# Two padding tiles: the raw weights and their low halves start 32 bytes later in SBUF, everything behind them 128 bytes later

## The reference

```
h = x
proj = rms_norm(h) @ w_in            # 1024 x 2048, 1024 x 4096, 1024 x 7584
... branches ...
h = h + y @ w_out                    # 1024 x 1024
f = rms_norm(h) @ [w_gate, w_up]     # 1024 x 2816 each
h = h + (silu(gate) * up) @ w_down   # 2816 x 1024
```

## The kernel before

| tile | start before | mod 64 | mod 256 |
|---|---|---|---|
| `weights_raw`, `weights_lo`, `weights_near` | 16576 | 0 | 192 |
| `weights_hi` | 41152 | 0 | 192 |
| `act_F_hi`, `act_F_lo` | 104064, 112256 | 0 | 128 |
| `ffn_F_hi`, `ffn_F_lo` | 120448, 142976 | 0 | 128 |
| `conv_F_hi`, `conv_F_lo` | 193152, 197248 | 0 | 128 |
| `mla_F_hi`, `mla_F_lo` | 122624, 126720 | 0 | 0 |
| `weights_hi_more`, `weights_raw_more` and `weights_lo_more` | 208576, 216768 | 0 | 192 |
| `z_T` | 128640 | 0 | 128 |
| `a_probs_T`, `v_T` (plain float32) | 171648, 136832 | 0 | 128 |
| `r_qk_F` (plain float32) | 193056 | 32 | 32 |
| `conv_acc_F` | 139488 | 32 | 224 |

## Time and profile before

### The profile page before, as it was taken

One profiled execution on the slowest core, in us unless ns is written; L12 is line 12 of the kernel. 1 busy time (PEld: TensorE's weight loads), 2 busy tenths in 40 slices (PEclk: granted clock), 3 DMA queues, 4 the chain that ended last, 5 costly groups with the idle time before them and its releaser, 6 DMA issues.

```text
span 1235.8 us, 19035 instructions
## 1 busy us (share of the span) xinstructions
PE 1205.2 (98%) x7597; PEld 1013.5 (82%) x7597; DVE 901.5 (73%) x1463; ACT 639.1 (52%) x1034; POOL 100.4 (8%) x163
## 2 busy tenths in 40 slices
PE   7999999999999999999999999999999999999998
PEld 3566778888988788787999987988788787999986
DVE  7998877757589998687666655589997687665553
ACT  4334565665556665545444544556575545444441
POOL 6300011101000200201000001000200201000000
PEclk9999999999999999999999999999999999999999
DMA  7635666434565555354766664565445355565552
GB/s 251 221 94 173 205 208 191 156 119 146 163 205 168 155 157 187 133 169 164 216 201 188 193 195 154 174 211 169 158 153 188 132 170 170 190 197 193 191 194 75
DMA packets 71958, 215.68 MB, mean 175 GB/s; under 512 B 16256, under 2 KB 19744, under 8 KB 71744
## 3 DMA queue, kind: packets, MB, share of 16 engines
q1 hardware_dynamic: 65008, 206.37, 52.0%
q0 software_dynamic: 2112, 6.97, 1.8%
q10 hardware_dynamic: 4752, 1.14, 0.4%
HBM read 208.95 MB, written 3.15 MB: 172 GB/s over the span
## 4 chain that ended last, share of the span: by engine, by line
PE 86%; DVE 8%; ACT 3%; issue 2%; POOL 1%; DMA 0%; DVEq 0%; POOLq 0%; ACTq 0%
PE acc L700 17%; PE acc L702 17%; PE acc L701 17%; PE acc L678 7%; PE acc L680 7%; PE acc L679 7%; PE acc L639 3%; PE mixed L1015 1%; DVE weights_lo L1776 1%; PE mixed L1112 1%; ACT junk L1279 1%; PE turned L755 1%; DVE h_T L1806 1%; PE mixed L999 1%; PE mixed L1008 1%
## 5 line engine op out<-in xcount | busy, mean ns | idle before, releaser
L1776 DVE TENSOR_TENSOR weights_lo<-weights_raw,weights_hi 128x1024 fp32r<-128x1024 f32 (+1 forms) x304 | 355.7, 1204 | 71.6 <-ACT weights_hi L1244 71.0
L1244 ACT ACTIVATE weights_hi<-weights_raw 128x1024 fp32r<-128x1024 f32 (+1 forms) x304 | 305.8, 1043 | 80.8 <-DMA weights_raw<-stream_dram 80.6
L700 PE MATMUL acc<-weights_hi,act_F_hi 128*128 128x512 f32 (+1 forms) x680 | 275.7, 406 | 5.6 <-DVE act_F_lo L1806 3.4
L702 PE MATMUL acc<-weights_hi,act_F_lo 128*128 128x512 f32 (+1 forms) x680 | 267.2, 393 | 0.0
L701 PE MATMUL acc<-weights_lo,act_F_hi 128*128 128x512 f32 (+1 forms) x680 | 265.4, 390 | 0.0
L678 PE MATMUL acc<-act_F_hi,weights_hi 128*128 128x256 f32 x624 | 173.6, 278 | 0.0
L679 PE MATMUL acc<-act_F_hi,weights_lo 128*128 128x256 f32 x624 | 172.5, 276 | 0.0
L680 PE MATMUL acc<-act_F_lo,weights_hi 128*128 128x256 f32 x624 | 172.4, 276 | 0.0
L700 PEld LDWEIGHTS acc<-weights_hi,act_F_hi 128*128 128x128 f32 x680 | 128.7, 189 | 34.2 <-DVE act_F_lo L1806 4.3
L702 PEld LDWEIGHTS acc<-weights_hi,act_F_lo 128*128 128x128 f32 x680 | 128.4, 189 | 28.4
L701 PEld LDWEIGHTS acc<-weights_lo,act_F_hi 128*128 128x128 f32 x680 | 128.7, 189 | 25.6
(11 more groups left out here) (339 smaller groups left out, 1923.6 us busy)
## 6 DMA issues: line engine op xcount, KB each, us to landing
weights_raw<-stream_dram SPq DMA_DIRECT2D x306, 512.0 KB, 3.7
weights_raw_more<-stream_dram SPq DMA_DIRECT2D x58, 512.0 KB, 4.3
gains<-rows_dram POOLq DMA_DIRECT2D x12, 512.0 KB, 4.8
weights_raw<-stream_dram SPq DMA_DIRECT2D x6, 416.0 KB, 3.1
weights_raw<-stream_dram SPq DMA_DIRECT2D x4, 384.0 KB, 3.5
x_T<-x_in_dram SPq DMA_DIRECT2D x4, 256.0 KB, 6.0
ssm_bc<-ssm_bc_dram SPq DMA_DIRECT2D x1, 1024.0 KB, 8.6
u_scratch<-u_T ACTq DMA_DIRECT2D x4, 256.0 KB, 5.5
```

What stands on the lines that cost most here:

```text
L700: pe.matmul(o, xh, wh, start=first and kk == 0, stop=False)
L702: i = pe.matmul(o, xl, wh, start=False, stop=last and kk == s["nk"] - 1)
L1244: act.activation(high(s, slice(0, n)), whole(s, slice(0, n)), ACT.Copy).then_inc(hi_made, 1)
L1776: dve.tensor_tensor(low(s, slice(0, n)), whole(s, slice(0, n)), high(s, slice(0, n)).bitcast(F32), ALU.subtract).then_inc(lo_made, 1)
```

## The change

Two lines change. The empty tile ahead of the weights grows from 64 to 96 bytes, and a new empty tile of 96 bytes stands between the low and the high halves.

```diff
-        sb("weights_offset", [P, 16])
+        sb("weights_offset", [P, 24])
         with ExitStack() as s0:
             sb("weights_near", [P, R0, SLOT], F32, s0)
             bcq = sb("ssm_by_pair", [P, 4, Q, GROUP], F32, s0)
         with ExitStack() as s0:
             raw = sb("weights_raw", [P, R, SLOT], F32, s0)
         w_lo = sb("weights_lo", [P, R, SLOT], F32R)
+        sb("weights_hi_offset", [P, 24])
```

## The result

| | before | after |
|---|---|---|
| median of 4 runs, us | 1237.6 | 1247.21 |
| lowest and highest, us | 1236.53, 1239.09 | 1245.92, 1247.78 |
| span of the profiled execution, us | 1235.8 | 1246.0 |

The changed kernel is slower: the ratio is 1.0077, 95% interval 1.0064 to 1.009, which is 9.6 us on the medians and 10.2 us on the spans. The forecast of 3.9 us has the right sign and less than half the size.

The account below looks back on a forecast made before the run. PE, streaming six matmul lines, was taken to bound the kernel. Terms 3.9 + 0 + 0 + 0 + 0 = 3.9 us, added to 1236.9, gave 1240.8 us; the range was 1233 to 1255 us.

Parts of the forecast that it names:

- PE is the path and only its rate matters: Whole kernel: PE busy 1205.2 of 1235.8 us at 2.4 GHz, so the streaming rate of six lines sets the end.
- The distance between the operands sets the rate: Matmuls: streamed against stationary start modulo 256 sets the rate; -64 costs 4.3 ns per matmul more than +64.
- The common 128 bytes cost 0: High halves and activations move together, keeping their distances, so L700, L702, L678 and L680 cost 0.
- Low half streamed, 896 x 4.3 = 3.9 us: L701: 896 matmuls streaming the low half slow by 4.3 ns each, 3.9 us, all on the path.
- Low half stationary, 624 x 0 = 0: L679 in `hidden_slot`: 624 matmuls with the low half stationary cost 0, bounds 4.2 and -4.2 us.
- The first 16 slots, within 0.3 us: L639, streaming `weights_raw` in plain float32: taken as 0, bound 0.3 us either way.
- make_lo, loads, ScalarE 0: VectorE's `make_lo`, ScalarE's copy and the loads: each taken as 0; loads at most 1.9 us if landings were 10% later.
- What would show it: Timeline test: six triples go from 4.12 to about 4.15 us; if `_more` places or `hidden_slot` move, distance isn't the cause.
- Straddling: Rival: streams starting at 32 touch two 64-byte lines per group; 16.1 us at full effect, 1253 us, chance 0.18.
- nothing: Rival: the rate depends on neither distance nor straddled lines; 1236.9 us, give or take 0.2%, chance 0.24.
- the remainder itself: Rival: a stationary tile starting at remainder 0 modulo 256 is slow, whatever the distance; 11.8 us, 1248.7 us, chance 0.06.

Follow-up runs that it names:

- the map: TensorE alone, not the full kernel: low and high halves each shifted in 32-byte steps, 8 x 8 pairs, in both matmul shapes; 340 to 373 ns per triple in `hidden_slot`'s shape.
- the third kernel of TensorE alone: TensorE alone, 20 stretches of slots at good and bad distances, behind each other and behind none to four transposes; good slots of `hidden_slot`'s shape took 340 or 353 ns.
- the last one: Kernel before the change with only `ffn_F`, `mla_F` and `conv_F` moved, to distance 0 from the weights; ratio 0.9994, 1236.5 against 1237.12 us.
- the one of 1242.2 us: Profiled execution of the kernel before with all tiles 32 bytes later, the first line of the change alone; measured ratio 1.0009.

## Why the prediction was right in sign and wrong in size

- *PE is the path and only its rate matters.* Held: PE's busy time grew by 10.1 of 10.2 us. The clock was not "at the higher level in every slice", though: the digits of the earlier trace rows hide two stretches of 3.4 us at 1.2 GHz, which lengthen the profile of before by 3.1 us.
- *The distance between the operands sets the rate.* Held, and shown by the shifts by 128 and by 32 bytes (1.0 and 1.0009) against those of one half (1.0149). That streamed reads and weight loads collide was argued, not shown. The rule that PE never waits on anyone (the Trainium skill, SBUF — State Buffer, section "Who interferes with whom") would make the change worth nothing. It speaks of other engines and is not refuted as such, but it could not price this change: in the map PE is alone, and its rate runs from 340 to 373 ns.
- *The common 128 bytes cost 0.* Held.
- *Low half streamed, 896 x 4.3 = 3.9 us.* Too small a price on too many matmuls. On `ffn_F` the triple grew by 13 ns, not 4.3, since -32 is not priced like -64 (map: 700 against 691); 144 of them gave 1.7 us. Of the 680 triples of `act_F` about a third grew by the same 13 ns, which outside the stretches at 1.2 GHz is 2.7 us. In all `tile_slot` gave 5.5 us outside them, against the forecast's 3.9, and 2.4 with them: that the latter is below the forecast is luck of the clock. Why the other triples on `act_F` stayed near 687, though their distances are the same as on `ffn_F`, isn't settled; in the third kernel of TensorE alone too -32 gave 687 in one series and 700 in others.
- *Low half stationary, 624 x 0 = 0.* This is the step that failed. It measured 6.5 us on its own places, and 7.0 with the extra ones, above its upper bound of 4.2. There were two errors in it. The value 0 was taken since nothing beyond the floor was visible at the old distance; but the old distance is one of three in 64 at which the map saw nothing, so the row could not speak for any other. And the bound counted only the matmuls on the low half, 624 of 1872, while all three matmuls of a triple grew by 3 to 4 ns. Had the prediction priced `hidden_slot` by the 13 ns that one bad distance was known to cost a triple of the other shape, it would have had 624 x 13 = 8.1 us here.
- *The first 16 slots, within 0.3 us.* +0.6 us by the starts, 620 ns mean against 615. The same line has 609 to 619 in the eight other kernels, in no order of their addresses, and 609 in the last one, where its addresses are those of before. No cost of the change is shown.
- *make_lo, loads, ScalarE 0.* Held to 1 ns, 0.1 us and 3 us of waits.
- *What would show it.* Extra places kept their rate (170 of 208 triples at 340). But that the distance is not the cause if `hidden_slot` moves was a wrong test. It moved, and the distance is the cause; and in the kernel with the low half at 0 even the extra places moved, at unchanged distances. A prediction that says what would refute it has to leave room for the part of the mechanism that no row has shown.
- *Rivals.* Straddling falls by the 32-byte shift of everything; "nothing" by the ratio; the remainder itself by the 128-byte shift, although its time, 1248.7, came nearest to the measured one. A right time is no evidence for its mechanism.

What stays open: which reads collide, if it is that, and so why 76 and 88 bytes are good and 72 and 80 are not; and what picks one of the rates that a distance allows. The runs give a table of rates, not a rule that yields them.

## What to carry to other kernels

Where TensorE streams back to back in float32r, the start of the streamed tile against that of the stationary one was worth up to 6% of the rate in these kernels, and the alignment of either by itself nothing that these runs could tell. Move operands that meet in a matmul together, or measure the pair of distances in a small kernel of TensorE alone before moving one: the medians of the map agree with those of every kernel here to 3 ns a triple. Measure each pair more than once, behind different work, since one series can show either of two rates. And before two sums of one line are compared, compare the granted clock of their stretches: here 3.1 us of clock hid a cost of the same size. And when a cost isn't visible in a row, ask first whether that row could be the one lucky point, and bound it by the worst that any other shape shows, counted on every instruction beside the moved operand.

## What was not expected of the hardware

- At 2.4 GHz streaming 256 columns took no less than 113.3 ns (340 / 3), with 32, 64 or 128 stationary columns and at every distance tried; 512 columns no less than 226.7 (680 / 3). Both are 17/16 of 106.7 and 213.3 ns, one column per cycle at 2.4 GHz.
- At 1.2 GHz this is gone: 512 columns took 426.7 ns (1280 / 3) in the two stretches of before, exactly one column per cycle of 1.2 GHz. So the extra cycle in 16 columns, which the prediction tied to 64 bytes of the stream, is not paid at the lower clock. The first stretch of the map suggests the same for the distance: both halves at 0, it begins with three triples of 640 ns, 3 x 256 columns at 1.2 GHz, and goes on at 360; its profile has no row for the clock at that point.
- Above that floor the rate depends on the distance of the operands: 340 to 373 ns per triple of 256 columns, 680 to 714 per triple of 512.
- At a good distance there are two stable rates, 340 and 353 ns, for 30 triples on end. Four transposes ahead gave either, and what chooses is open. Part of the difference between executions comes from this: the one of 1242.2 us had 209 more triples at 353 on main places, which is 2.7 of its 6.4 us over the span of before.
- With a stationary tile of 64 columns instead of 128 the good distance and the bad one changed places (340 and 360 ns became 357 and 340), in one series each.
